# Hybrid decoder step on one core: filler projections spread by TensorE columns instead of by steps

## The chip, the cores and the metric

The kernel runs on one core of a Trainium2 chip. The metric is the time of one execution on the device in microseconds (us). Engines are called as in the profile: PE is the matrix engine (TensorE), PEld its weight loads, DVE is VectorE, ACT is ScalarE, POOL is GpSimd, SP is SyncE, which issues all the transfers (DMA) here.

## What is computed

Two layers of a decoder. Each normalises 1024 prompt rows and 64 sample rows of width 1024, multiplies them by one wide input matrix, and takes from the product queries, keys and values (8 heads of 64), gates, and the inputs of a second mixer. The first mixer is causal attention with a decay:

```
s = q k^T * scale + (c_q - c_k)      c = cumulative sum of log forget gates
s = -inf above the diagonal
p = softmax(s);  out = p v
m = sigmoid(g_a) * (a @ w_pa) + sigmoid(g_b) * (b @ w_pb);  x = x + m @ w_o
```

Everything is in f32 precision: an operand is split into a high and a low part, and a product is three matmuls (high by high, high by low, low by high) of at most 512 columns, in the helper `three` (L71, L72, L73).

## The kernel before

The program is a sequence of phases: constants, normalisation of rows, and then for each layer attention, spatial, branches, merge and output. The change touches one function, `attention_plan` (L461), which writes down by hand the order of the attention phase. Every engine walks through the same list of steps in `attention_phase` (L541) and does its own part of each, in that order; semaphores tie them together. The kinds of steps that matter:

- **T(h, G, j)**, **V(h, G, j)**: head h, query half G (512 queries), key block j. T transposes up to four 128x128 blocks of the softmax result (L1089). ACT copies them out of the bank as the high part (L810), DVE subtracts for the low part (L991). V multiplies by the values (L1102, L1103), LAG = 2 steps after its T. There are 96 of these steps for each layer, 12 for each head; "step n" below counts them from 0, so head h starts at step 12h. Step n issues T of step n and V of step n - 2.
- **S(h, i)**: scores of the query block i (L1072, L1074, L1077). DVE adds the decay and takes the maximum (L975), ACT does the exponential (L800), DVE normalises (L877). A chunk of scores waits on PE until DVE has taken the chunk two before it. S of head h + 1 goes beside T and V of head h.
- **O(h, G)**: after the last V of a group, ACT (L819) and DVE (L998) add the two halves of the result. The next group's first V (j = 0) waits for it on PE.
- **W(p, k)**: a weight tile for the heads of pair p: SP loads it (L653, L656), ACT makes the high part (L739), POOL the low part for even k (L838), DVE for odd k (L899). **Z(p, t)**: their projection, 24 matmuls of 384 columns, and **X(p, t)** its transposes (L1049). POOL works on each Z for its norm.
- **P(b, c, half)**: the filler. 16 blocks b of the merge gates, each of three column chunks c (384, 384 and 320 columns), are projected in two halves of 12 matmuls. After both halves ACT takes the tanh (**E**, L754), which frees the bank, and SP stores it (**D**, L679). 14 of the 96 halves run before step 0, and 82 beside the steps. Its weights come in **G** units, two for each b: SP loads them (L660, L662), ACT makes the high part (L746) and POOL the low part (L843).

W and G share a ring of NST = 4 staging slots. In the order of the plan, the load of unit u + 4 is issued when SP gets to unit u, and `load_w` (L646) first waits until unit u has been split into high and low. G units of block b + 2 come into the plan behind the last half of block b, so wherever that half is moved, they go along.

The filler is dealt out by the loop at the end of `attention_plan`. A half costs 1 and a Z costs 2; the other kinds cost nothing. After each step it adds halves until what was spent has caught up with an equal share for each step:

```
total = sum(2 * (s[0] == "Z") ...) + len(fill.pieces) - first
while spent + fill.at - first < total * (n + 1) / (len(steps) + 1) and ...:
    fill.half()
```

That is 54 for the 27 Z and 82 halves, 136 in all, or 1.4 for each step. Before a Z an open pair is closed by its second half (`before_z`, L449).

Of the kernel before, what the change touches and what calls it, by code (L numbers as in the profile page):

```python
# [26 lines left out]
KT = D // P  # L27
# [430 lines left out]
        self.spill(0)  # L458


def attention_plan():  # L461

    plan = [("W", 0, k) for k in range(KT)]
    fill = Filler(plan)
    for t in range(NT):  # L470
        plan.append(("Z", 0, t))
        if t:
            plan.append(("X", 0, t - 1))
        if t >= 3:
            fill.weights(min(t - 2, NF))
    plan += [("F",)]
    fill.chunk()
    plan += [("W", 1, k) for k in range(2)]
    fill.chunk()
    plan += [("X", 0, NT - 1), ("C",), ("N", 0)]  # L480
    for i in range(1, 4):
        plan += [("W", 1, k) for k in (2 * i, 2 * i + 1)]
        fill.chunk()
    fill.read(0)
    plan += [("S", 0, 0), ("S", 0, 1)]
    fill.half()
    plan += [("S", 0, 2)]
    fill.half()
    fill.read(0)
    plan += [("S", 0, 3)]  # L490
    fill.half()
    fill.half()
    after = {}
    PER = 12

    def put(n, *steps):
        after.setdefault(n, []).extend(steps)

    for h in range(H):
        if h:  # L500
            put(PER * (h - 1), ("N", h))
        for i, off in enumerate((-10, -9, -8, -6, -4, -3, -2, 0)):
            if h or i >= 4:
                put(max(0, PER * h + off), ("S", h, i))
    for p in range(1, PAIRS):
        at = [3, 5, 7, 9, 11, 13, 15, 17, 19]
        for t, n in zip(range(NT - len(at), NT), at):
            n += 2 * PER * (p - 1)
            put(n, ("Z", p, t))
            if t and ("X", p, t - 1) not in plan:  # L510
                put(n, ("X", p, t - 1))
        put(n + 2, ("X", p, NT - 1))
        if p + 1 < PAIRS:
            for k in range(KT):
                put(n + 1 + k // 2, ("W", p + 1, k))
    steps = [(h, G, j) for h in range(H) for G in range(2) for j in range(4 * G + 4)]
    first = fill.at
    total = sum(2 * (s[0] == "Z") for v in after.values() for s in v) + len(fill.pieces) - first
    spent = 0
    for n in range(len(steps) + LAG):  # L520
        if n < len(steps):
            plan.append(("T",) + steps[n])
        fill.read(0)
        if n >= LAG:
            plan.append(("V",) + steps[n - LAG])
            h, G, j = steps[n - LAG]
            if j == 4 * G + 3:
                plan.append(("O", h, G))
        for s in after.pop(n, []):
            if s[0] == "Z":  # L530
                fill.before_z()
                spent += 2
            plan.append(s)
        while spent + fill.at - first < total * (n + 1) / (len(steps) + 1) and fill.at < len(fill.pieces):
            fill.half()
    fill.end()
    assert not after
    return plan


def attention_phase(nc, l, g, sem):  # L541
    plan = attention_plan()
    R = Region(nc, "at", g.free_attention)
    S = lambda n: sem(f"a_{n}")
# [1513 lines left out]
```

How the kernel before makes its waits and increments, by code:

```python
        @block.sync  # L103
        def _(sp):
            for t in range(NT):
                if t >= NX:
                    sp.wait_ge(hn_r, t - NX + 1)
                    sp.wait_ge(ss_r, t - NX + 1)
                sp.dma_start(xt[0:ROWS[t], t % NX, :], x_rows(g, t)).then_inc(x_in[t % NX], 16)
                if t == 1:
                    sp.dma_start(gain[:, :], g.gains[0:1, :].to_broadcast([P, D])).then_inc(consts, 16)
# [1 line left out]
        @block.scalar  # L113
        def _(act):
            def evac(t):
                for b in range(2):
                    act.wait_ge(tr_r, t + 1)
                    nc.scalar.activation(g.h_hi[:, 4 * b:4 * b + 4, t * P:t * P + ROWS[t]],
                                         hps[t % 2][b][:, :].rearrange("p (k r) -> p k r", k=4)[:, :, 0:ROWS[t]],
                                         ACT.Copy).then_inc(h_hi, 1)
            for t in range(NT):
                act.wait_ge(x_in[t % NX], 16 * (t // NX + 1))
                if t:
                    act.wait_ge(ss_r, t)
                    if t >= 2:
                        act.wait_ge(ms_r, t - 1)
                nc.scalar.activation(sqj[0:ROWS[t], :], xt[0:ROWS[t], t % NX, :], ACT.Square,
                                     accum_out=ss[0:ROWS[t], t % 2:t % 2 + 1]).then_inc(ss_r, 1)
                if t:
                    evac(t - 1)
            evac(NT - 1)
# [12 lines left out]
        @block.vector  # L145
# [13 lines left out]
                if t:  # L159
                    evac(t - 1)
                dve.wait_ge(ss_r, t + 1)
                if t >= 2:
```

## Time and profile before

| what | value |
|---|---|
| median of three runs (2157.60 to 2164.94) | 2157.71 us |
| the profiled execution: its own time, its span | 2161.27 us, 2159.6 us |
| PE busy, share of the span | 1941.4 us, 90% |
| DVE, ACT, POOL busy | 981.4, 678.0, 486.1 us |
| mean granted clock of PE | 0.965 |
| filler matmuls (three lines), busy | 261.1 + 254.6 + 254.5 us |

The span is the time from the first to the last instruction of the profiled execution. Matmuls overlap and their ends are modelled, so busy time says where PE had something in hand, while the distance from start to start says how fast it went. A group's "idle before" is the time its engine stood before these instructions, with what released it. Idle time costs something only on the engine that sets the pace. The steps run from 159.4 to 578.4 us in layer 0 and from 1213.5 to 1629.7 us in layer 1.

### The profile page before, as it was taken

The page shows a single profiled execution, that of the slowest core. Times are in us where ns is not written, and L with a number is a line of the kernel's source. Part 1 is how long each engine was busy: PE and PEld are TensorE (multiplying, and loading weights), DVE is VectorE, ACT ScalarE, POOL GpSimd, SP SyncE. Part 2 cuts the span into 40 slices and gives each one's busy share as a digit, 9 for nine tenths or more (in the row PEclk, how much of TensorE's full clock was granted, in tenths as well). Part 3 has the DMA queues.
Part 4 walks back from the last instruction along what each step waited for, and adds up shares of the span by engine and source line. Part 5 has one row for each costly group of instructions (what it writes and reads, how often), then busy time and mean ns, then how long its engine had stood idle before and what let it go on. Part 6 is the DMA issues. An engine that isn't in the chain of part 4 may idle for free. (4 is left out here: it accounts for less than half of the span.)

```text
span 2159.6 us, 31030 instructions
## 1 busy us (share of the span) xinstructions
PE 1941.4 (90%) x11188; PEld 1780.0 (82%) x11188; DVE 981.4 (45%) x2322; ACT 678.0 (31%) x1487; POOL 486.1 (23%) x499
## 2 busy tenths in 40 slices
PE   2789989999896999898979898999997789989899
PEld 2689888999775889897859898989996588889876
DVE  3335646554255324444434365565533633344441
ACT  3233434444232322103223343443433232221020
POOL 0432323331111112202015132333211021121010
PEclk9999999999997999999989999999999899999999
DMA  2341231212213322433222313131212152214341
GB/s 92 71 102 43 57 80 51 78 52 78 77 47 93 112 83 67 156 108 127 103 63 59 103 47 81 48 92 49 70 47 81 39 152 84 72 51 154 107 166 59
DMA packets 215499, 178.38 MB, mean 83 GB/s; under 512 B 50004, under 2 KB 186724, under 8 KB 215348
## 3 DMA queue, kind: packets, MB, share of 16 engines
q1 hardware_dynamic: 215348, 176.41, 28.3%
q8 instruction: 90, 1.47, 0.3%
q14 instruction: 61, 0.50, 0.1%
HBM read 131.65 MB, written 44.71 MB: 82 GB/s over the span
## 5 line engine op out<-in xcount | busy, mean ns | idle before, releaser
L71 PE MATMUL bank<-keep_hhi,at_fhi 128*128 128x384 f32 (+1 forms) x768 | 261.1, 340 | 16.2 <-ACT at_th L754 16.2
L73 PE MATMUL bank<-keep_hhi,at_flo 128*128 128x384 f32 (+1 forms) x768 | 254.6, 331 | 0.0
L72 PE MATMUL bank<-keep_hlo,at_fhi 128*128 128x384 f32 (+1 forms) x768 | 254.5, 331 | 0.0
L71 PE MATMUL bank<-at_whi,keep_hhi 128*128 128x384 f32 (+3 forms) x576 | 201.3, 349 | 17.6 <-POOL at_wlo L838 17.5
L71 PE MATMUL bank<-keep_hhi,br_whi 128*128 128x384 f32 (+1 forms) x576 | 196.2, 341 | 20.6 <-POOL br_wlo L1109 20.6
L72 PE MATMUL bank<-at_wlo,keep_hhi 128*128 128x384 f32 (+3 forms) x576 | 198.0, 344 | 0.0
L73 PE MATMUL bank<-at_whi,keep_hlo 128*128 128x384 f32 (+3 forms) x576 | 197.7, 343 | 0.0
L72 PE MATMUL bank<-keep_hlo,br_whi 128*128 128x384 f32 (+1 forms) x576 | 189.7, 329 | 0.0
L73 PE MATMUL bank<-keep_hhi,br_wlo 128*128 128x384 f32 (+1 forms) x576 | 189.5, 329 | 0.0
L800 ACT ACTIVATE at_prob<-at_prob,at_nmx 128x128 f32<-128x128 f32 (+7 forms) x128 | 99.5, 777 | 280.4 <-DVE at_nmx L982 280.3
L991 DVE TENSOR_TENSOR at_ptlo<-bank,at_pthi 128x512 fp32r<-128x512 f32 x192 | 106.0, 552 | 157.6 <-ACT at_pthi L810 157.6
L71 PEld LDWEIGHTS bank<-keep_hhi,at_fhi 128*128 128x128 f32 x768 | 147.1, 191 | 19.8 <-ACT at_th L754 17.6
L72 PEld LDWEIGHTS bank<-keep_hlo,at_fhi 128*128 128x128 f32 x768 | 147.3, 192 | 0.8
L73 PEld LDWEIGHTS bank<-keep_hhi,at_flo 128*128 128x128 f32 x768 | 146.8, 191 | 0.0
L843 POOL TENSOR_TENSOR at_flo<-at_stage,at_fhi 128x512 fp32r<-128x512 f32 x64 | 82.0, 1292 | 241.5 <-ACT at_fhi L746 241.5
L71 PE MATMUL bank<-wo_whi,keep_hhi 128*128 128x512 f32 (+1 forms) x288 | 116.3, 404 | 14.2 <-POOL wo_wlo L1109 14.2
L71 PEld LDWEIGHTS bank<-keep_hhi,br_whi 128*128 128x128 f32 x576 | 109.5, 190 | 22.7 <-POOL br_wlo L1109 21.1
L71 PEld LDWEIGHTS bank<-at_whi,keep_hhi 128*128 128x128 f32 (+1 forms) x576 | 106.9, 186 | 23.7 <-POOL at_wlo L838 20.9
L810 ACT ACTIVATE at_pthi<-bank 128x512 fp32r<-128x512 f32 x192 | 93.7, 488 | 94.6 <-PE bank L1089 94.1
L72 PE MATMUL bank<-wo_wlo,keep_hhi 128*128 128x512 f32 (+1 forms) x288 | 115.1, 400 | 0.0
L73 PE MATMUL bank<-wo_whi,keep_hlo 128*128 128x512 f32 (+1 forms) x288 | 115.1, 400 | 0.0
L851 POOL TENSOR_TENSOR at_zg<-at_zc,at_gqk 128x256 f32<-128x256 f32 (+1 forms) x72 | 53.0, 736 | 266.4 <-ACT at_zc L763 266.4
(240 smaller groups left out, 4406.2 us busy)
## 6 DMA issues: line engine op xcount, KB each, us to landing
mg_gate<-gates SPq DMA_DIRECT2D x32, 544.0 KB, 7.0
at_stage<-in_w_in SPq DMA_DIRECT2D x128, 128.0 KB, 2.6
at_stage<-in_w_in SPq DMA_DIRECT2D x64, 192.0 KB, 2.7
gates<-at_th SPq DMA_DIRECT2D x64, 192.0 KB, 2.3
br_stage<-in_w_in SPq DMA_DIRECT2D x48, 256.0 KB, 3.2
at_decay<-ncum SPq DMA_DIRECT2D x16, 512.0 KB, 4.1
br_k<-in_cache_k SPq DMA_DIRECT2D x32, 256.0 KB, 3.0
br_v<-in_cache_v SPq DMA_DIRECT2D x32, 256.0 KB, 3.0
```

Source lines behind the costliest of these rows:

```text
L71: nc.tensor.matmul(out, sh, mh, start=start and i == 0, stop=False)
L72: nc.tensor.matmul(out, sh, ml, start=False, stop=False)
L73: last = nc.tensor.matmul(out, sl, mh, start=False, stop=stop and i == n - 1)
L800: nc.scalar.activation(prob[:, blk(i):blk(i) + w], prob[:, blk(i):blk(i) + w], ACT.Exp, bias=nmx[:, si % 2:si % 2 + 1], accum_out=sm[:, si ...
L810: nc.scalar.activation(pt_hi[:, ti % (LAG + 1), lo:512], tps[ti % 2][:, lo:512], ACT.Copy).then_inc(t_hi, 1)
L843: nc.gpsimd.tensor_tensor(flo[:, fu % NF, :], stage[:, units[s] % NST, :], fhi[:, fu % NF, :].bitcast(F32), ALU.subtract).then_inc(w_lo_p, 1)
L851: link(nc.gpsimd.tensor_tensor(zg[0:n, :].rearrange("p (s h d) -> p s h d", s=2, h=2), zc[0:n, zi % 2, 0:2 * P].rearrange("p (s h d) -> p ...
L991: nc.vector.tensor_tensor(pt_lo[:, ti % (LAG + 1), lo:512], tps[ti % 2][:, lo:512], pt_hi[:, ti % (LAG + 1), lo:512].bitcast(F32), ALU.sub ...
```

## The change

The halves are dealt out by columns that pass through PE, with every kind of step counted. The list of other steps, and their order among themselves, stays; only P and what hangs on it (E, D, G) moves.

```diff
+HALF = 12 * 384.0
+def cost(s):
+    if s[0] == "Z":
+        return 3 * KT * 384.0
+    if s[0] == "X":
+        return 4 * 240.0
+    if s[0] == "S":
+        return (s[2] // 4 + 1) * 2 * 400.0 + 128
+    if s[0] == "T":
+        h, G, j = s[1:]
+        return (4 - max(0, j - 4 * G)) * 200.0
+    if s[0] == "V":
+        h, G, j = s[1:]
+        return (4 - max(0, j - 4 * G)) * 2 * 128.0
+    return 0.0
...
-    total = sum(2 * (s[0] == "Z") for v in after.values() for s in v) + len(fill.pieces) - first
-    spent = 0
+    total = sum(cost(s) for v in after.values() for s in v) + sum(cost(("T",) + s) + cost(("V",) + s) for s in steps)
+    total += HALF * (len(fill.pieces) - first)
+    spent = 0.0
     for n in range(len(steps) + LAG):
         if n < len(steps):
             plan.append(("T",) + steps[n])
+            spent += cost(plan[-1])
         fill.read(0)
         if n >= LAG:
             plan.append(("V",) + steps[n - LAG])
+            spent += cost(plan[-1])
...
             if s[0] == "Z":
                 fill.before_z()
-                spent += 2
             plan.append(s)
-        while spent + fill.at - first < total * (n + 1) / (len(steps) + 1) and fill.at < len(fill.pieces):
+            spent += cost(s)
+        while spent + HALF * (fill.at - first) < total * (n + 1) / (len(steps) + 1) and fill.at < len(fill.pieces):
             fill.half()
```

Worked through, the total is 865,216 columns, and a step's share 8,920. Halves issued in each step (the same in both layers):

| steps | before | after |
|---|---|---|
| 0 to 7 | 2 1 2 1 0 0 0 0 | 1 2 1 0 1 1 0 0 |
| 8 to 19 | 1 1 0 0 1 1 0 0 0 0 1 1 | 0 0 1 1 0 0 0 0 1 1 0 0 |
| 20 to 27 | 0 1 2 1 2 1 1 0 | 0 1 2 1 2 1 2 1 |
| 28 to 37 | 1 1 0 0 1 1 0 0 0 0 | 0 0 1 1 0 0 0 0 0 0 |
| 38 to 44 | 1 1 0 0 1 1 0 | 1 1 0 0 1 1 0 |
| 45 to 51 | 1 1 2 1 2 1 0 | 0 2 1 2 1 2 0 |
| 52 to 67 | 1 1 0 0 0 0 1 1 0 0 1 1 0 0 0 0 | 1 1 0 0 0 0 0 0 1 1 0 0 1 1 0 0 |
| 68 to 71 | 1 2 1 1 | 0 1 1 2 |
| 72 to 95 | 35 in all, 1 or 2 each | 38 in all, 1 to 3 each |

Z stands in every second step from 3 to 19, 27 to 43 and 51 to 67. The two G units of b = 6 move from step 23 to step 24, behind W(2, 7), which stays in step 23. Those of b = 8 move from step 43, ahead of all W(3, k) (steps 44 to 47), to step 46, between W(3, 5) and W(3, 6); with 4 staging slots the load of W(3, 6) is then issued at W(3, 4) and no longer at W(3, 2), and that of W(3, 7) at W(3, 5) and no longer at W(3, 3).

## Rows read from the trace of the kernel before

**Rows 1.** Stretches: us, busy (count) of PE PEld DVE ACT POOL, PEclk, DMA, GB/s

```profile
159.40:578.40 419.00, 402.64 (x2465) 384.14 (x2463) 219.18 (x636) 168.94 (x396) 115.45 (x113) 0.99 0.23 62
1213.50:1629.70 416.20, 401.19 (x2466) 382.68 (x2464) 219.07 (x636) 168.94 (x396) 115.42 (x113) 0.99 0.23 62
```

**Rows 2.** Waits of PE in the first stretch: total us, times, longest us

```profile
PE bank L1102 <- DVE at_ao L998: 7.1, 7, 3.0
PE bank L1072 <- DVE at_mx L975: 6.8, 8, 1.4
PE bank L71 <- ACT at_th L754: 2.5, 1, 2.5
```

**Rows 3.** The same view, second stretch

```profile
PE bank L1102 <- DVE at_ao L998: 7.0, 7, 3.0
...
PE bank L71 <- ACT at_th L754: 0.9, 1, 0.9
```

**Rows 4.** Timeline of PE: start us, us, engine, line, operation [idle before <-releaser]

```profile
270.84 0.39 PE L71 MATMUL bank<-keep_hhi,at_fhi 128*128 128x384 f32 x1
...
272.98 0.34 PE L71 MATMUL bank<-keep_hhi,at_fhi 128*128 128x384 f32 x1
```

**Rows 5.** Timeline of PE at score steps, without and with work between them

```profile
370.57 0.47 PE L1072 MATMUL bank<-at_qk 128*128 128x512 f32 x1 [1.17 <-DVE at_mx L975]
...
419.58 0.40 PE L1103 MATMUL bank<-at_ptlo,at_vsplit 128*128 128x512 f32 x1
421.40 0.47 PE L1072 MATMUL bank<-at_qk 128*128 128x512 f32 x1 [1.42 <-DVE at_mx L975]
...
474.25 0.40 PE L1103 MATMUL bank<-at_ptlo,at_vsplit 128*128 128x512 f32 x1
474.48 0.40 PE L1072 MATMUL bank<-at_qk 128*128 128x512 f32 x1
```

**Rows 6.** Timeline of PE at the first value product of a group

```profile
242.75 0.47 PE L1102 MATMUL bank<-at_pthi,at_vsplit 128*128 128x512 f32 x1 [0.80 <-DVE at_ao L998]
...
445.50 0.47 PE L1102 MATMUL bank<-at_pthi,at_vsplit 128*128 128x512 f32 x1 [1.10 <-DVE at_ao L998]
...
463.31 0.47 PE L1102 MATMUL bank<-at_pthi,at_vsplit 128*128 128x512 f32 x1 [0.31 <-DVE at_ao L998]
```

**Rows 7.** Timeline of all engines, 271 to 284 us, head 2 of layer 0

```profile
271.07 0.38 SPq L660 DMA_DIRECT2D at_stage<-in_w_in  x1
...
271.59 1.20 DVE L899 TENSOR_TENSOR at_wlo<-at_stage,at_whi 128x392 fp32r<-128x392 f32 x1
...
274.17 0.63 ACT L746 ACTIVATE at_fhi<-at_stage 128x512 fp32r<-128x512 f32 x1 [2.71 <-DMA at_stage<-in_w_in]
...
276.75 0.63 ACT L746 ACTIVATE at_fhi<-at_stage 128x512 fp32r<-128x512 f32 x1 [1.95 <-DMA at_stage<-in_w_in]
...
278.25 0.44 PE L71 MATMUL bank<-keep_hhi,at_fhi 128*128 128x384 f32 x1 [2.52 <-ACT at_th L754]
...
283.78 0.76 PE L1102 MATMUL bank<-at_pthi,at_vsplit 128*128 128x512 f32 x1 [2.96 <-DVE at_ao L998]
```

**Rows 8.** Stretch table at the low granted clock

```profile
283.20:290.00 6.80, 6.22 (x20) 5.96 (x21) 1.76 (x7) 0.83 (x5) 0.00 (x0) 0.50 0.24 71
1338.00:1341.40 3.40, 3.40 (x13) 3.31 (x12) 0.59 (x4) 0.82 (x4) 0.00 (x0) 0.51 0.18 61
```

**Rows 9.** Timeline of all engines, 375 to 392 us, heads 3 and 4

```profile
375.28 0.47 PE L1072 MATMUL bank<-at_qk 128*128 128x512 f32 x1 [0.36 <-DVE at_mx L975]
...
382.90 2.65 POOL L838 TENSOR_TENSOR at_wlo<-at_stage,at_whi 128x392 fp32r<-128x392 f32 x2 [3.88 <-ACT at_whi L739]
...
383.68 0.95 ACT L739 ACTIVATE at_whi<-at_stage 128x392 fp32r<-128x392 f32 x2
...
384.77 1.20 DVE L899 TENSOR_TENSOR at_wlo<-at_stage,at_whi 128x392 fp32r<-128x392 f32 x1
...
391.77 0.47 PE L1102 MATMUL bank<-at_pthi,at_vsplit 128*128 128x512 f32 x1 [0.49 <-DVE at_ao L998]
```

## The prediction

> **What bounds the kernel now.** I read the stretch table first, for the attention steps alone. PE is busy for 402.6 of 419.0 us in layer 0 and 401.2 of 416.2 in layer 1, while DVE has work for about 219 [rows 1]. So PE sets the pace and only some 16 and 15 us of each stretch are open to a new order: moving halves cannot shorten PE's own work. Next I read who PE waits for: seven waits for DVE's sum of the two output halves (V with j = 0, behind O), eight for DVE's reading of a score bank, and one for a tanh that frees the filler's bank [rows 2, 3]. Everything outside the attention phase is issued as before, so it costs nothing either way: no cover of it is touched.
>
> The profiled execution took 2161.27 us with a span of 2159.6; the median of three is 2157.71. The sum is made against the profiled execution and then put on the median, 3.56 us lower.
>
> **What a half is worth.** One half starts at 270.84 and the next at 272.98, so a 384-column half takes 2.14 us of PE [rows 4]. All 82 are still issued. What counts is what PE waits for where one is gone, and which wait is covered where one has come. A wait costs a little more than its listed idle time, as ends are modelled: from the second V matmul to the scores it is 1.82 us with an idle time of 1.42, and 0.23 us without a wait, so 1.59 are lost, 0.17 more than listed [rows 5]. I add 0.2 to every listed wait.
>
> **Scores behind scores.** In steps 8 and 32 the half goes that stands between S(h, 4) and S(h, 5), with a Z ahead of both. Steps 56 and 57 have this very order already: PE is through with its V at once and waits 1.42 us for DVE, which is still at the Z's share. That makes 1.6 us at each of the two places. In step 68 it is the same with the shorter last Z (64 rows); the like place after step 44 waited 1.17 [rows 5], so 1.4. Sum **+4.6** for each layer.
>
> **Values behind O.** With a Z but no half since the last step but one, the first V of the next group waited 1.10 us in step 62 and 0.80 in step 18 [rows 6]; where halves stand in both steps ahead (steps 12 and 13, ahead of step 14) there is no wait. The change takes the halves of 12 and 13 away (+1.3 in step 14), and gives two to 16 and 17 (-1.0 in step 18) and to 60 and 61 (-1.3 in step 62). One wait of 0.31 goes in step 66 [rows 6] and one of the same kind comes in step 30. Sum **-1.0**.
>
> **Head 2, steps 24 to 27.** Here is the longest idle time. ACT reaches the G units of b = 6 before their loads have landed and stands for 2.71 and 1.95 us; the tanh, the copies of T and O queue behind it, and PE idles 2.52 us ahead of P(5, 1, 0) and 2.96 ahead of V(2, 0, 0) [rows 7]. In layer 1 the first is 0.9, the second again 3.0 [rows 3]. The change puts these units a step later, behind the exponential of S(2, 7). Then T(2, 0, 0) is copied at once. DVE is done with W(2, 7) at 271.59 + 1.20 = 272.8 [rows 7]. From the like point of heads 3 and 4 (384.77 + 1.20 = 385.97) to the first V (391.77) it took 5.8 us [rows 9]; two G copies and a tanh now lie in this chain, 2 x 0.63 [rows 7] and about 0.5, so V(2, 0, 0) starts at 272.8 + 5.8 + 1.75 = 280.3. PE gets there at about 277.9, so it waits 2.4 where it lost 2.7 + 3.2. That is **-3.5** in layer 0 and, from 1.1 + 3.2, **-1.9** in layer 1. The granted clock fell to its lower level (0.50 of 2.4 GHz) for 6.8 us in layer 0 and 3.4 us in layer 1, right behind this idle time [rows 8]. At half speed such a stretch loses half of itself, less the idle part: 3.1 and 1.7. With one wait of 2.4 us left I count 0.3 of it as still there: **-2.8** and **-1.4**.
>
> **Heads 3 and 4, steps 45 to 50.** The half behind S(4, 5) goes. S(4, 6) waits for DVE to read S(4, 5), which hangs on DVE's queue (copy of T, split of W), not on PE; it starts at 375.28 after a wait of 0.36 [rows 9] and would start then with one half less done: **+2.1**. Then the weights. W(3, 6) is now loaded only when W(3, 4) is split. POOL's two splits from 382.90 take 2.65 us together [rows 9], so the first ends at 384.2. A load needed 3.1 us from its issue (271.07) to its use (274.17), the next one was ready 2.6 later [rows 7]. So W(3, 6) is there at about 387.4 and W(3, 7), issued 0.9 later, at 388.3 at the earliest and 390.0 at the latest; I take 388.3, as this stretch has no stores of Z beside it. ACT copies them at 383.68 today, without a wait [rows 9]. Behind ACT's wait stand the copy of T(4, 0, 0), the exponential of S(4, 7), the copy of T(4, 0, 1), one tanh and O; DVE waits at W(3, 7) with the low parts and the scores behind it. POOL and SP wait too, but what they hold (loads of b = 10, the decay row of head 5) is needed later. DVE's split ends at 388.3 + 0.5 + 1.2 = 390.1 and no longer at 385.97; with the 5.8 us chain and the tanh, V(4, 0, 0) starts at 396.4. PE has done the same number of halves by then as before (six since S(4, 6)), so it arrives at 391.0 as today and waits 5.4 us where it lost 0.7: **+4.6**. The clock: an idle time of this length should let it fall. The stretches above cost 1.7 and 3.1 [rows 8]; I take 2.0 here and 0.8 for the 2.7 us ahead of S(4, 6): **+2.8**.
>
> The Trainium skill, page "DMA: Bandwidth & Descriptors", section "Anatomy of one DMA — SWDGE (gpsimd) path", gives a transfer about 2.0 us and its bytes at 436 GB/s, which would be an estimated 2.45 us for such a load; that is for another issuing path. By it both loads would land 0.65 us sooner and the sum be about 1.3 us smaller.
>
> **Sum.** Layer 0: 4.6 - 1.0 - 3.5 - 2.8 + 2.1 + 4.6 + 2.8 = +6.8. Layer 1: 4.6 - 1.0 - 1.9 - 1.4 + 2.1 + 4.6 + 2.8 = +9.8. Together +16.6: the profiled execution would take 2177.9 us, and the median **2174.3 us**, 0.77% slower. A change within 0.5% (10.8 us) is about what a measurement of this kernel can't tell from none.
>
> **Bounds.** The landing of W(3, 7) is worth 1.7 us more in each layer if late and 0.5 less if early. The clock is worth from 0 to 3.1 at each place; from no fall at either place to one of 3.1 at both: -2.8 to +3.4. Two layers: 2167.7 to 2184.5.
>
> **Rivals.** (a) *The weights come in time.* If ACT has other work until the loads land, or V(4, 0, 0) is held by nothing new, 4.6 and the 2.0 of clock fall away in each layer: +3.4 in all, 2161.1 us. For it speaks that no wait of ACT for W shows at these steps today, against it that the ring's slot is freed only at 384.2 and the use is at 383.7 today. (b) *The two old clusters only change places*, with all smaller waits as before: 2157.7 us, or what amounts to the change not doing what it says, since Z and the weight steps keep their places and the halves shift by one to four steps. (c) *Faster.* DVE's lag behind a Z, 1.42 us at S, decides. Should it be gone when fewer tanhs and stores run beside it, neither the score waits (4.6), nor S(4, 6) (2.1), nor head 4 (4.6 and 2.8) come, and what is saved in head 2 stays: 16.6 - 2 x 14.1 = -11.6, 2146.1 us. It needs a lag under some 0.2 us. Against it: the lag comes from DVE's and ACT's own instructions, which don't change, and was there at each of eight S waits [rows 2]. (d) *Slower still*: the second load comes 1.7 us late, the clock falls at three places in each layer for 3.1 each instead of 3.1 in all (counting the 0.3 in head 2): 16.6 + 2 x (1.7 + 6.2) = +32.4, 2190.1 us.
>
> **Chances.** The forecast 0.65; (a) 0.14, (b) 0.09, (c) 0.05, (d) 0.07. Below 10.8 us of change lie (a), (b) and a small part of the forecast's own range (0.04 of it): same 0.27, faster 0.05, slower 0.68. The range takes in the forecast's bounds and (b) with a little scatter, and stops short of (c) and of the far end of (d): 2156 to 2186.
>
> **What would show it.** In the profile after: no wait of ACT for the load of at_fhi and 2.4 us of PE idle, not 5.5, in head 2; PE's clock at 1.0 there; new waits of L1072 for L975 of 1.4 us in steps 9, 33 and 69; 2.5 us or more ahead of S(4, 6); ACT's L739 waiting 2 to 4 us for a load of at_stage, and a wait of some 5 us at L1102 for L998 in head 4, the longest in the steps, with a fall of the clock beside it. The forecast is wrong if that last wait is under 2 us, or if PE's idle time in the steps grows by less than 3 us in each layer.

## The result and the profile after

The change makes the kernel slower: 2174.69 us median against 2158.7 for the kernel before on the same chip, a ratio of 1.007, with a 95% interval of 1.0051 to 1.0089. The profiled execution of after took 2173.97 us with a span of 2172.3, against 2161.27 and 2159.6 before. So the forecast (2174.3 us, 0.77% slower) held; by the medians the change costs 16.0 us, by the two profiled executions 12.7.

First the stretch table of after, for the steps of layer 0 and of layer 1, and three short stretches in layer 0 at the low granted clock. The columns are those of [rows 1].

```profile
160.30:584.90 424.60, 403.52 (x2465) 384.67 (x2464) 219.00 (x636) 168.33 (x396) 115.48 (x113) 0.99 0.22 61
1219.60:1643.10 423.50, 403.00 (x2464) 384.19 (x2463) 218.95 (x636) 168.44 (x396) 115.53 (x113) 0.99 0.22 61
371.10:374.50 3.40, 3.40 (x12) 3.22 (x13) 1.63 (x6) 2.79 (x7) 0.74 (x1) 0.50 0.40 93
391.60:395.00 3.40, 3.40 (x15) 3.40 (x14) 0.91 (x5) 0.49 (x2) 0.00 (x0) 0.50 0.51 154
333.60:337.00 3.40, 3.40 (x13) 3.30 (x12) 1.78 (x8) 0.49 (x2) 1.94 (x2) 0.50 0.28 60
```

The steps are 424.6 and 423.5 us long where they were 419.0 and 416.2 [rows 1]: +5.6 and +7.3, 12.9 together, where the whole span grew by 12.7 (the rest of the program is the same within 0.3). PE's busy time grew by under 2 us, as half clock stretches count as busy; the rest is waiting. The low clock of head 2 [rows 8] is gone and stands now at heads 3 and 4.

Who PE waits for in the first stretch of after (total us, times, longest):

```profile
PE bank L1096 <- DVE at_mx L999: 13.5, 11, 2.5
PE bank L1126 <- DVE at_ao L1022: 7.5, 6, 2.5
```

L1096, L1126 and L71 of after are L1072, L1102 and L71 of before. The score waits were 6.8 us in eight and are 13.5 in eleven; the V waits are 7.5 where they were 7.1; the wait for a tanh is gone [rows 2]. The timeline of PE in layer 0 of after shows each kind once (S(1, 5), V(1, 0, 0), V(2, 0, 0), V(3, 0, 0), S(4, 6), V(4, 0, 0)):

```profile
203.71 0.47 PE L1096 MATMUL bank<-at_qk 128*128 128x512 f32 x1 [1.42 <-DVE at_mx L999]
...
228.50 0.47 PE L1126 MATMUL bank<-at_pthi,at_vsplit 128*128 128x512 f32 x1 [1.11 <-DVE at_ao L1022]
...
277.63 0.47 PE L1126 MATMUL bank<-at_pthi,at_vsplit 128*128 128x512 f32 x1 [1.41 <-DVE at_ao L1022]
...
332.31 0.47 PE L1126 MATMUL bank<-at_pthi,at_vsplit 128*128 128x512 f32 x1 [2.06 <-DVE at_ao L1022]
...
371.05 0.70 PE L1096 MATMUL bank<-at_qk 128*128 128x512 f32 x1 [2.47 <-DVE at_mx L999]
...
391.03 0.47 PE L1126 MATMUL bank<-at_pthi,at_vsplit 128*128 128x512 f32 x1 [2.47 <-DVE at_ao L1022]
```

Behind the last of them lie ACT, POOL and DVE at the weights of heads 3 and 4 (same kernel, same layer):

```profile
374.13 1.07 DVE L923 TENSOR_TENSOR at_wlo<-at_stage,at_whi 128x392 fp32r<-128x392 f32 x1 [0.60 <-ACT at_whi L763]
...
379.04 1.36 DVE L923 TENSOR_TENSOR at_wlo<-at_stage,at_whi 128x392 fp32r<-128x392 f32 x1
...
382.77 0.53 ACT L763 ACTIVATE at_whi<-at_stage 128x392 fp32r<-128x392 f32 x1 [2.24 <-DMA at_stage<-in_w_in]
383.38 1.04 POOL L862 TENSOR_TENSOR at_wlo<-at_stage,at_whi 128x392 fp32r<-128x392 f32 x1 [0.58 <-ACT at_whi L763]
...
384.10 0.53 ACT L763 ACTIVATE at_whi<-at_stage 128x392 fp32r<-128x392 f32 x1 [0.79 <-DMA at_stage<-in_w_in]
...
384.66 0.57 DVE L923 TENSOR_TENSOR at_wlo<-at_stage,at_whi 128x392 fp32r<-128x392 f32 x1 [4.06 <-ACT at_whi L763]
```

ACT copies W(3, 6) and W(3, 7) only when their loads land, and DVE stands 4.06 us for the second, where before it went straight on [rows 9].

To say how much each step cost I took, in both traces, the time from the start of each of its items to the start of the next, less what an item of that kind takes when nothing holds it. This gives the loss of PE by step, waits and half clock together (us, before to after):

| step | what is lost there | layer 0 | layer 1 |
|---|---|---|---|
| 9, 33, 69 | S behind S | 0.13, 0.13, 0.18 to 1.86, 1.85, 1.67 | the same to 1.84, 1.84, 1.66 |
| 14 | V(1, 0, 0) | 0.01 to 1.35 | 0.01 to 1.33 |
| 18, 62, 66 | V of a group | 1.10, 1.45, 0.55 to 0.01 each | 1.07, 1.45, 0.55 to 0.01 each |
| 25 to 27 | head 2 | 9.10 to 1.95 | 6.18 to 1.95 |
| 38, 39 | V(3, 0, 0) | 1.58 to 4.10 | 1.58 to 2.54 |
| 46 | S(4, 6) | 0.67 to 4.40 | 0.67 to 4.31 |
| 50 | V(4, 0, 0) | 0.84 to 4.38 | 0.84 to 4.22 |
| 86 | V(7, 0, 0) | 0.11 to 0.51 | 0.11 to 0.43 |

Step 0 is given apart, as its four scores wait for each other in every kernel: from the start of T(0, 0, 0) to the first half it takes 8.2 us in before and 7.6 in after in layer 0 (159.39 to 167.59, 160.34 to 167.93), and 8.3 in both in layer 1.

### The profile page after: what moved, and what is told of

It is laid out like the page before. It is cut to its first block and busy times, and to the rows that moved or that the text cites. A ratio compares the mean times of both kernels' runs of the same rounds, so it can differ in the third digit from the quotient of the medians.

```text
span 2172.3 us, 31030 instructions
## 1 busy us (share of the span) xinstructions
PE 1941.7 (89%) x11188; PEld 1779.5 (82%) x11188; DVE 979.7 (45%) x2322; ACT 677.0 (31%) x1487; POOL 486.9 (22%) x499
## 5 line engine op out<-in xcount | busy, mean ns | idle before, releaser
L71 PE MATMUL bank<-keep_hhi,at_fhi 128*128 128x384 f32 (+1 forms) x768 | 262.8, 342 | 13.1 <-ACT at_th L778 13.1
L71 PE MATMUL bank<-at_whi,keep_hhi 128*128 128x384 f32 (+3 forms) x576 | 200.1, 347 | 18.6 <-POOL at_wlo L862 17.9
L71 PE MATMUL bank<-keep_hhi,br_whi 128*128 128x384 f32 (+1 forms) x576 | 196.1, 341 | 20.5 <-POOL br_wlo L1133 20.5
L71 PEld LDWEIGHTS bank<-keep_hhi,at_fhi 128*128 128x128 f32 x768 | 148.9, 194 | 16.2 <-ACT at_th L778 14.2
L71 PE MATMUL bank<-wo_whi,keep_hhi 128*128 128x512 f32 (+1 forms) x288 | 115.8, 402 | 14.1 <-POOL wo_wlo L1133 14.1
L71 PEld LDWEIGHTS bank<-keep_hhi,br_whi 128*128 128x128 f32 x576 | 109.4, 190 | 22.6 <-POOL br_wlo L1133 21.1
L71 PEld LDWEIGHTS bank<-at_whi,keep_hhi 128*128 128x128 f32 (+1 forms) x576 | 106.2, 184 | 24.0 <-POOL at_wlo L862 20.3
```

What stands on the lines that cost most here:

```text
L71: nc.tensor.matmul(out, sh, mh, start=start and i == 0, stop=False)
```

## The experiments

Eleven kernels were run in three groups, each group on one chip with its own runs of the kernel before; ratios are to that. Each expectation spells out what its theories say. A is in most of them the working of the prediction, by which each loss belongs to the item named for it (in experiment 4 that is B, in the last three D). B is otherwise the rival of the text in question. C came up after the fifth kernel and stands in the last three. "Losses" are those of the table above.

**1. The two G units of b = 8 behind the exponential of S(4, 7)**, everything else as in after, so that W(3, 6) and W(3, 7) are loaded as early as before.

```
 # after, behind fill.end()
+units = [("G", 16), ("G", 17)]
+plan = [s for s in plan if s not in units]
+at = plan.index(("P", 7, 1, 0)) + 1      # end of step 48
+plan[at:at] = units
```

> The changed kernel, with only the two weight units of filler block 8 moved from step 46 to the end of step 48, behind the exponential of S(4,7), so that W(3,6) is loaded at W(3,2) again. Theory A (late loads): ACT's two waits for at_stage at W(3,6) and W(3,7), 2.2 and 0.8 us, go; the wait ahead of V(4,0,0), 2.7 us, falls to about 1, the clock doesn't fall behind it, and each layer saves about 3 us, 6 in all (span near 2166). Theory B (only one half stands between V(3,1,7) and V(4,0,0), where there were two): the wait stays at 2.5 us or more and the time stays within 1 us.

Measured: 2169.52 us, 1.0033 (1.0023 to 1.0043). Steps 419.6 and 419.5 us. In its timeline of PE, the first scores of group 1, S(4, 6) and V(4, 0, 0):

```profile
361.49 0.40 PE L1100 MATMUL bank<-at_qk 128*128 128x512 f32 x1
...
369.08 0.76 PE L1100 MATMUL bank<-at_qk 128*128 128x512 f32 x1 [2.46 <-DVE at_mx L1003]
...
386.51 0.47 PE L1130 MATMUL bank<-at_pthi,at_vsplit 128*128 128x512 f32 x1 [0.16 <-DVE at_ao L1026]
```

The wait ahead of V(4, 0, 0) is 0.16 where it was 2.47, and the half clock behind it is gone: step 50 loses 0.51 where it lost 4.38. S(4, 6) still waits 2.46. Theory A had 3 us less in each layer; it was 4 to 5. So the place of two small units, through the loads that queue behind them, was worth some 4 us in each layer.

**2. The same kind of edit on the kernel before**: the G units of b = 6 at the end of step 24, halves untouched.

```
 # before, behind fill.end()
+units = [("G", 12), ("G", 13)]
+plan = [s for s in plan if s not in units]
+at = plan.index(("D", 14)) + 1
+plan[at:at] = units
```

> The kernel before, with only the two weight units of filler block 6 moved from step 23 to the end of step 24. Theory A (what was gained in head 2 comes from these units' place alone): the wait ahead of P(5,1,0), 2.5 and 0.9 us, goes, that ahead of V(2,0,0) falls from 3.0 to about 1.5, the clock doesn't fall there; 7 us less in layer 0 and 4 in layer 1, so a span near 2148 and a ratio near 0.995. Theory B (the halves' own new places gained it): within 2 us of before.

Measured: 2153.29 us, 0.9953 (0.9941 to 0.9965). V(2, 0, 0) and the stretch of layer 0, from its timeline and stretch table:

```profile
279.74 0.47 PE L1106 MATMUL bank<-at_pthi,at_vsplit 128*128 128x512 f32 x1 [1.50 <-DVE at_ao L1002]
```

```profile
159.50:571.70 412.20, 399.59 (x2465) 381.25 (x2463) 219.06 (x636) 169.02 (x397) 115.80 (x113) 1.00 0.24 63
```

Head 2 lost 9.1 and 6.2 us and loses 2.0 in each layer, with the granted clock at 1.00 over the stretch. What the change gains in head 2 is this move alone; no half had to move for it.

**3. The halves back where a score step needs one.** The loop is replaced by a list of halves for each step, which is that of after but for steps 8 to 11, 30 to 33, 68 and 71.

```
-        while spent + HALF * (fill.at - first) < total * (n + 1) / (len(steps) + 1) and fill.at < len(fill.pieces):
+        while fill.at - first < sum(HALVES[:n + 1]):
             fill.half()
 # 8 to 11: 0 0 1 1 -> 1 1 0 0; 30 to 33: 1 1 0 0 -> 0 0 1 1; 68: 0 -> 1; 71: 2 -> 1
```

> The changed kernel, with a half put back between S(h,4) and S(h,5) in steps 8 and 32 (with its partner in 9 and 33, taken from 10, 11, 30 and 31) and one in step 68 (taken from 71). Theory A: the three waits of L1096 for L999, 1.4, 1.4 and 1.2 us, go and nothing takes their place: 4.9 us less in each layer, near 10 in all (span near 2162.5). Theory B (DVE's lag only moves to the next group): less than 4 us in all, with longer waits at the V that follow.

Measured: 2166.0 us, 1.0015 (1.0005 to 1.0026). The waits of PE in layer 0:

```profile
PE bank L1099 <- DVE at_mx L1002: 8.9, 8, 2.5
PE bank L1129 <- DVE at_ao L1025: 6.6, 6, 2.5
```

Score waits are eight again, 4.6 us less in all. The losses of steps 9, 33 and 69 went back to 0.13, 0.11 and 0.18. V(3, 0, 0) went back too: its listed wait is 1.11 again where after has 2.06, as two halves stand between S(3, 4) and V(3, 0, 0) again and PE comes there later. That answers to the 1 us which the prediction had not seen. The steps are 417.9 and 418.0 us long.

**4. One half from step 46 to step 45**, behind S(4, 5), where before had it.

```
 # after with HALVES; 45: 0 -> 1; 46: 2 -> 1
```

> The changed kernel, with one of the two halves of step 46 put back into step 45, between S(4,5) and S(4,6). Theory A (DVE's chain and the late loads fix when V(4,0,0) starts): the wait ahead of S(4,6) falls from 2.5 to 0.4 us and the clock doesn't fall there, but what the clock gives back is lost again as a longer wait ahead of V(4,0,0), near 4 us; only the half itself is gained, 2.1 us in each layer, 4.2 in all (span near 2168). Theory B (the waits add up freely): 3.7 us in each layer, 7.4 in all (span near 2165).

Measured: 2178.43 us, 1.0068 (1.0052 to 1.0084). S(4, 6) and V(4, 0, 0) in its timeline of PE:

```profile
370.48 0.47 PE L1099 MATMUL bank<-at_qk 128*128 128x512 f32 x1 [0.68 <-DVE at_mx L1002]
...
390.64 0.77 PE L1129 MATMUL bank<-at_pthi,at_vsplit 128*128 128x512 f32 x1 [4.63 <-DVE at_ao L1025]
```

The wait at S(4, 6) went from 2.47 to 0.68 and that at V(4, 0, 0) from 2.47 to 4.63; step 46 loses 0.98 in place of 4.40, step 50 loses 7.19 in place of 4.38, and both stretches are as long as in after or longer (424.7 each). Nothing was won, where the two theories had 2.1 and 3.7 us in each layer. A wait that is filled without anything crossing the next one is only handed on.

**5. Experiments 1 and 4 together.** No new lines beside theirs.

> Both edits of e1 and e4 in the changed kernel: the weight units of filler block 8 behind step 48, and a half back in step 45. e4 alone gained nothing, since no half had moved across V(4,0,0), whose start the late loads fixed. Theory A (with the loads early, DVE's chain from S(4,6) sets V(4,0,0), and a half between S(4,5) and S(4,6) is done for nothing): the waits ahead of S(4,6) and V(4,0,0) come to about 0.6 and 0.7 us as in the kernel before, no fall of the clock in steps 45 to 50; against e1 3.3 us less in each layer, span near 2162. Theory B (V(4,0,0) is fixed by something else): the time of e1, within 2 us of a span of 2168.7.

Measured: 2176.61 us, 1.0075 (1.0059 to 1.0092): a clear miss, a loss beside experiment 1 (1.0033) where a gain was expected. Its timeline of PE and stretch table:

```profile
363.80 0.40 PE L1103 MATMUL bank<-at_qk 128*128 128x512 f32 x1
...
388.84 0.77 PE L1133 MATMUL bank<-at_pthi,at_vsplit 128*128 128x512 f32 x1 [3.22 <-DVE at_ao L1029]
```

```profile
388.50:391.90 3.40, 3.06 (x11) 2.90 (x12) 1.18 (x6) 0.75 (x3) 0.39 (x1) 0.50 0.96 284
391.90:395.30 3.40, 3.40 (x15) 3.40 (x14) 0.34 (x2) 0.63 (x1) 0.63 (x1) 0.51 0.39 136
```

The loads are early, so V(4, 0, 0) starts 25.0 us behind S(4, 4), just as in experiment 1 (361.49 to 386.51). What PE no longer waits at S(4, 6) (3.2 us of loss less) it waits at V(4, 0, 0) (3.3 more); and behind this wait the clock is low for 6.8 us, in which the first items of step 50 lose 2.8 us.

**What these five say together (theory C).** From S(4, 4) to V(4, 0, 0) runs a chain of DVE and ACT: scores read, exponentials, low parts, splits of W, tanh, O, the sum at at_ao. It has a length of its own. PE's items in it take 5.9 us and 2.14 for each half [rows 4]; the rest of the length is lost, wherever inside it shows. (Two of the halves inside have 320 columns and take about 1.8 us; the 5.9 allows for them. In experiments 9 and 10 it is three, and 5.55.) Measured in layer 0, with the same chain in head 2:

| kernel, head | S(h, 4) to V(h, 0, 0), us | halves inside | PE loses |
|---|---|---|---|
| before, 2 | 29.26 | 7 | 8.41 |
| before, 4 | 24.10 | 7 | 3.24 |
| after, 2 | 25.00 | 7 | 4.15 |
| after, 4 | 27.57 | 6 | 8.80 |
| 1, head 4 | 25.02 | 6 | 6.24 |
| 3, head 4 | 27.53 | 6 | 8.77 |
| 4, head 4 | 27.78 | 6 | 9.01 |
| 5, head 4 | 25.04 | 6 | 6.26 |

(27.57 - 5.9 - 6 x 2.14 = 8.8 for after; 24.10 - 5.9 - 7 x 2.14 = 3.2 for before.) The half of experiment 4 moved inside the chain, so the loss stayed. What the edit of the spreading rule did was to move one half out of the chain of head 4, behind V(4, 0, 0), and to lengthen the chain by 3.5 us.

This holds for heads 2 and 4, which have the W splits and no Z in the span. In head 3, with three Z in it, the same span follows the halves (26.25 us with two in before, 24.67 with none in after), so its length is not set by the other engines.

**6. Experiments 1, 3 and 4 together**, as one kernel.

> The changed kernel with the edits of e1, e3 and e4 together; what remains of the change is the place of the block 6 units, and halves moved to 16, 17, 60, 61, 64, 65. Theory A (the three costs are separate and sum up): about 12 us less lost than in the changed kernel in each layer (3.9, 4.9 with 1 at V(3,0,0), 3.4): a span near 2149, ratio to the kernel before near 0.995, like e2. Theory B (they overlap): span above 2155.

Measured: 2159.26 us, 0.9999 (0.9989 to 1.001), where 2149 was hoped for. Steps 415.6 and 415.5 us. The chain of head 4 is 25.04 with six halves and loses 6.29, as in 5. Experiment 4's edit gains nothing, and the gains of 1 and 3 come but for 1.5 us in each layer: steps 46 and 50 together lose 6.1 where they lose 4.6 in experiment 1, since most of the waiting stands ahead of V(4, 0, 0) again and the clock falls behind it (0.50 from 383.1 to 386.5).

**7. Only the late loads, put into the kernel before**: the G units of b = 8 between W(3, 5) and W(3, 6), halves of before.

```
 # before, behind fill.end()
+units = [("G", 16), ("G", 17)]
+plan = [s for s in plan if s not in units]
+at = plan.index(("W", 3, 5)) + 1
+plan[at:at] = units
```

> The kernel before, its halves untouched, with only the two weight units of filler block 8 moved from step 43 to step 46, between W(3,5) and W(3,6). Theory A (late loads alone cost it): ACT waits about 2 and 1 us for at_stage at W(3,6) and W(3,7), the wait ahead of V(4,0,0) grows from 0.7 to near 4 us, the clock falls behind it: 4 to 6 us in each layer, span near 2169, ratio near 1.0045. Theory B (it needs the missing halves too): ratio under 1.002.

Measured: 2171.27 us, 1.0049 (1.0032 to 1.0066). The chain of head 4 grew from 24.10 to 27.67 (27.64 in layer 1) with its seven halves; step 50 loses 5.63 and 3.26 where it lost 0.84, step 49 a further 0.9. So the late loads cost without any half moved. The stretches grew by 7.8 and 1.6 us. Theory A had 4 to 6 in each layer and a span near 2169; the profiled one is 2169.3. Layer 0: some 6.4 in steps 48 to 51 (of these 1.9 behind V(4, 0, 0), by the clock) and 1.6 at step 0. Layer 1: 3.6 in steps 48 to 50, less 1.9 in head 2, whose order is not changed: what head 2 loses varies from one execution to the next.

**8. A version made by these rules from the kernel before.** No step's place but that of halves and G units is changed.

```
 # before with HALVES
 # a pair from each of 18, 38, 58, 62 to 16, 36, 56, 60; a new pair in 64, 65;
 # one half from 26 to 20 and one from 50 to 44; one less in 77 and in 87
+for units, last in (([("G", 12), ("G", 13)], ("T", 2, 0, 1)), ([("G", 18), ("G", 19)], ("T", 4, 0, 1))):
+    plan = [s for s in plan if s not in units]
+    at = plan.index(last)
+    plan[at:at] = units
```

> The kernel before with the halves dealt out by a list, put where PE waits: pairs from 18, 38, 58 and 62 to 16, 36, 56 and 60, a new pair at 64, one half from 26 to 20 and one from 50 to 44, two fewer after step 76; the weight units of blocks 6 and 9 behind S(2,7) and S(4,7). Theory A (each wait is covered by a half ahead of it): the waits of 0.8 to 1.4 us in steps 18, 21, 38, 45, 57, 62 and 66 go, head 2's too; 17 us less in layer 0 and 14 in layer 1, span near 2129, ratio near 0.986. Theory B (DVE and ACT are then what bounds these steps, and the waits come back one step later): less than half of that, ratio above 0.993.

Measured: 2133.16 us, 0.9869 (0.9852 to 0.9886). Steps 405.6 and 404.0 us, 13.4 and 12.2 less than in before, where theory A had 17 and 14. The chains of heads 2 and 4 are 25.07 and 25.01 long and hold eight halves, and lose 2.0 to 2.1.

**9. One half from step 50 to step 45 in after**: now one does cross V(4, 0, 0).

```
 # after with HALVES; 45: 0 -> 1; 50: 2 -> 1
```

> The changed kernel, with one half taken from step 50, behind V(4,0,0), and put into step 45. e4 moved one within the stretch from S(4,4) to V(4,0,0) and gained nothing. Theory C (that stretch is one chain through DVE and ACT, 24.1 us in the kernel before, 27.6 with the late loads, and PE's wait is what of it the halves inside don't fill, wherever they stand in it): the stretch stays at 27.6 us, and with seven halves inside in place of six the waits of steps 46 and 50 together fall by 2.1 us, 2 to 3 us less in each layer, span near 2167.5. Theory D (each wait stands for itself): the wait of S(4,6) falls by 2.1 us and the clock no longer falls ahead of V(4,0,0), whose wait stays at 2.7: 3.7 us in each layer, span near 2165.

Measured: 2173.54 us, 1.0064 (1.0046 to 1.0082).

```profile
361.83 0.40 PE L1099 MATMUL bank<-at_qk 128*128 128x512 f32 x1
...
389.30 0.47 PE L1129 MATMUL bank<-at_pthi,at_vsplit 128*128 128x512 f32 x1 [3.24 <-DVE at_ao L1025]
```

389.30 - 361.83 = 27.47: the length stands, with seven halves it loses 6.94 in place of 8.80, and layer 0 is 1.9 us shorter than in after. Layer 1 is only 0.7 shorter; there the clock fell behind V(3, 0, 0), where it had not in after. By theory C 2 to 3 us in each layer were expected.

**10. The same, and the G units of b = 8 behind O**, at the end of step 49.

```
 # experiment 9, and behind fill.end()
+units = [("G", 16), ("G", 17)]
+plan = [s for s in plan if s not in units]
+at = plan.index(("P", 7, 2, 0)) + 1
+plan[at:at] = units
```

> As e9, and the two weight units of filler block 8 out of the chain altogether, to the end of step 49 behind O(3,1). Theory C: the stretch from S(4,4) to V(4,0,0) is back at 24.1 us with seven halves inside, the waits of S(4,6) and V(4,0,0) at 0.6 and 0.7 us, no fall of the clock: 7 us less than the changed kernel in each layer, span near 2158, ratio near 1.000. Theory D: as e9 plus the 3.9 us that e1 gained in each layer, the same total by another road; so the lengths of the stretch in e9 and e10 tell the two apart, not the time here.

Measured: 2164.52 us, 1.002 (1.0008 to 1.0032). The chain is 24.10 us long in layer 1, with step 50 at 0.85. In layer 0 it is 25.31, and the timeline of PE and ACT says why:

```profile
363.37 0.40 PE L1103 MATMUL bank<-at_qk 128*128 128x512 f32 x1
...
386.70 0.49 ACT L785 ACTIVATE at_th<-bank 128x384 f32<-128x384 f32 x1 [1.18 <-DMA gates<-at_th]
387.21 0.59 ACT L850 ACTIVATE at_ao<-bank 64x512 f32<-64x512 f32 x1
...
388.68 0.47 PE L1133 MATMUL bank<-at_pthi,at_vsplit 128*128 128x512 f32 x1 [1.71 <-DVE at_ao L1029]
```

A tanh ahead of O's copy waits 1.18 us until a store has read its buffer: 24.10 + 1.18 = 25.28. The steps are 5.6 and 6.7 us shorter than in after, where 7 were expected, and the time stays above the expected 1.000.

**11. Experiment 8 with both pairs of G units behind O**, and the pair of halves of steps 42, 43 in 40, 41.

```
 # experiment 8, with
-([("G", 12), ("G", 13)], ("T", 2, 0, 1)), ([("G", 18), ("G", 19)], ("T", 4, 0, 1))
+([("G", 12), ("G", 13)], ("T", 2, 0, 3)), ([("G", 18), ("G", 19)], ("T", 4, 0, 3))
```

> As e8, with the weight units of blocks 6 and 9 behind O, out of the chain to V(2,0,0) and V(4,0,0) (in e8 they stood between the exponential and O), and the pair of steps 42 and 43 in 40 and 41. Theory C: both chains are about 1 us shorter, the waits ahead of V(2,0,0) and V(4,0,0) fall from 1.6 and 1.5 to 0.6 and 0.5 us, that of step 42 from 1.0 to 0: about 3 us less in each layer than e8, ratio near 0.984. Rival: the copies were hidden behind DVE's work, and the time stays at e8's ratio of 0.987.

Measured: 2131.06 us, 0.9863 (0.9845 to 0.988), the best, though no further below experiment 8 than the intervals allow. Its timeline of PE, its waits and its stretch table, all of layer 0:

```profile
355.62 0.40 PE L1079 MATMUL bank<-at_qk 128*128 128x512 f32 x1
...
379.73 0.47 PE L1109 MATMUL bank<-at_pthi,at_vsplit 128*128 128x512 f32 x1 [0.33 <-DVE at_ao L1005]
```

```profile
PE bank L1079 <- DVE at_mx L982: 2.9, 3, 1.4
PE bank L1109 <- DVE at_ao L1005: 0.9, 3, 0.4
```

```profile
161.10:561.80 400.70, 396.67 (x2465) 380.72 (x2463) 219.03 (x636) 168.70 (x398) 115.53 (x113) 1.00 0.24 65
```

The chain is 24.11 us (379.73 - 355.62) and loses about 1.1 with eight halves. Outside step 0 PE loses 2.9 us less in each layer than in experiment 8, which is what theory C had. PE is busy for 396.7 of 400.7 us, with 3.8 us of listed waits where before had 16.4 [rows 2]. In layer 1 the stretch is some 2 us longer, all of it in step 0, where the clock fell (0.50 from 1201.0 to 1207.8) and in layer 0 did not; that hides part of the gain in the time.

## Why the prediction was right, and which term was off

The total was right in direction and size, and by the terms that carried it, but that it agrees to 0.4 us is luck. The steps grew by 12.9 us in the traces where the sum has 16.6. V(4, 0, 0) and head 2 came out smaller than forecast, and a loss at V(3, 0, 0) that was not seen makes up for part of it. The rest is scatter: the four times of after span 4.2 us and the four of before 7.3, and their medians happen to lie 16.0 apart. Forecast and measured, by layer:

| step of the prediction | forecast | layer 0 | layer 1 |
|---|---|---|---|
| scores behind scores | +4.6 | +4.9 | +4.9 |
| values behind O | -1.0 | -1.7 | -1.7 |
| head 2, waits and clock | -6.3 / -3.3 | -7.2 | -4.2 |
| S(4, 6), V(4, 0, 0) and clock | +9.5 | +7.3 | +7.0 |
| V(3, 0, 0) | 0 | +2.5 | +1.0 |
| V(7, 0, 0), step 0 | 0 | -0.2 | +0.3 |
| steps in all | +6.8 / +9.8 | +5.6 | +7.3 |

- *Scores behind scores* was right in place and size (1.42 listed, 1.7 lost at steps 9 and 33), and experiment 3 took all three back by giving the halves back.
- *Values behind O*: the four places of steps 14, 18, 62 and 66 behave as said; the wait at step 30 that would have cost 0.3 did not come, and step 66 gave back 0.5 instead of 0.3.
- *Head 2*: the mechanism was right, as experiment 2 shows alone. ACT finds the loads of G there: its two copies start at once behind the exponential (trace of after, 274.31), with no wait. The wait ahead of V(2, 0, 0) is 1.41 listed and not 2.4, because the two G copies and the tanh do not add 1.75 us to the chain: with the G units in it the chain is 25.0 where without it is 24.1, so 0.9. And the clock stayed up, so nothing of its cost was left.
- *Heads 3 and 4*: the loads landed as forecast: ACT's copy of W(3, 7) started 13.05 us behind S(4, 6) (371.05 to 384.10), the forecast being 388.3 - 375.28 = 13.0. **The term that was mis-sized is V(4, 0, 0), +4.6 (its own figures, 5.4 less 0.7, give 4.7); it measured +2.0** (+1.8 in layer 1), three steps of its working being off. DVE's split took 0.57 us, not 1.2, as POOL's own had ended at 384.42. The tanh was not on the chain: ACT did it from 388.98 to 389.46, while DVE normalised, and from the split's end (385.23) to V (391.03) it is the 5.8 us of before. And PE did not "arrive at 391.0 as today": the half clock behind S(4, 6), from 371.1 to 374.5, made it 1.7 us later. That half clock loss lies inside a chain whose length DVE and ACT set, so it was counted twice: once as clock, once in the wait it shortens. S(4, 6) was right (2.0 for 2.1), the clock roughly so (0.8 + 0.9 behind S(4, 6) and 1.6 behind V(4, 0, 0), 3.3 for 2.8).
- *Not seen*: V(3, 0, 0), 1 us more in each layer. Two halves are gone between S(3, 4) and V(3, 0, 0), and the forecast has a price only for the scores behind S(3, 4) (experiment 3 gives both back). In layer 0 there is a fall of the clock behind it, 1.4 us; in layer 1 the clock did not fall behind the same wait. V(7, 0, 0) adds 0.4 and 0.3. Against them, at step 0 of layer 0 the clock fell in the trace of before (163.8 to 167.2) and not in that of after: 0.6 us that no edit explains.
- *The signs*: the wait ahead of V(4, 0, 0) was to be some 5 us and the longest. It is 2.47, level with S(4, 6), and not far above the 2 us under which the forecast called itself wrong. ACT waits 2.24 and 0.79 us for the two loads where 2 to 4 was said. PE's idle time in the steps (length less busy) grew by 4.7 and 5.5 us, over the 3 that were asked for.
- *The rivals*: (a), the weights in time, is what experiment 1 makes of the change: its steps are 0.6 and 3.4 us longer than those of before where (a) has 0.2 and 3.2, so the total of (a) fits a kernel with early loads, and the change is not one. Its parts fit less well: V(3, 0, 0) is in none of them, and head 2 came out smaller. (b) is excluded by the eleven score waits. (c) needed DVE's lag to vanish; it is 1.42 us, as before. Of (d) only the fall at V(3, 0, 0) came, in one layer.
- *The figure of the Trainium skill* (page "DMA: Bandwidth & Descriptors", section "Anatomy of one DMA — SWDGE (gpsimd) path"): 2.0 us and the bytes at 436 GB/s, an estimated 2.45 us, would have had both loads ready 0.65 us earlier than the 3.1 us taken from the rows. In the trace W(3, 6) was issued at 380.00 and used at 382.77, W(3, 7) at 380.94 and 384.10: 2.8 and 3.2 us, so the time from the rows is the nearer one. The two are for different issuing paths.

## What to carry to other kernels

An even spread of filler by cost is not better than one by number of steps if it does not know where the waits are (here it was 0.7% worse): find the spans whose length another engine's chain sets, measure them between two anchors, and count how much work PE has inside; an item moved within such a span gains nothing, one moved into it gains its duration as long as that much of the span is left (here up to eight halves, which left about 1.1 us). Outside such spans each wait wants a half ahead of it, as at the scores behind a Z. What is left over goes where PE waits for nothing. Before moving a small unit that holds a slot of a staging ring, look which load is issued when that slot comes free, and what stands in order behind the instruction that will wait for it: here two G units behind W(3, 5) cost 3.5 us of chain in each layer, and two others behind an exponential gave 4 to 7 back. Waits that are given as separate terms must be checked for lying in one span, half clock included.

## What the runs showed of the hardware that was not expected

- DVE's subtraction of two 128x392 tiles takes 0.57 us with POOL idle (each of the eight such in after), and 1.07, 1.36 and 1.20 us beside the same operation of POOL (374.13 and 379.04 in after; [rows 9]). With the second price on the path, a split may be cheaper where both engines are not at it together. The Trainium skill, page "GPSIMD Engine Reference", section "Specifications", says that POOL's SBUF interfaces are shared with VectorE's, with contention where a DVE instruction has two SBUF inputs, as this one has; the trace agrees.
- A fall of the clock costs by where it lies. In experiment 1 the clock fell at S(4, 6) (3.4 us from 368.6), inside the chain, which is none the longer for it (25.02 us, and 25.04 in experiment 5, where it did not fall there). In experiment 5 the same total of waiting stood in one piece at the chain's end, the clock fell behind it for 6.8 us from 388.4, and 2.8 us were lost in each layer on top.
- Behind the same wait of 2.06 to 2.08 us at V(3, 0, 0) the clock fell in some layers and not in others; each such fall cost 1.4 to 1.6 us of PE. It went together with step 0. Six kernels have this wait (after and experiments 1, 4, 5, 9 and 10). In seven of their twelve layers the clock had not fallen in the scores of step 0 (7.6 us from T(0, 0, 0) to the first half), and in all seven it fell behind V(3, 0, 0). In the other five it had fallen there (8.2 to 8.3 us), and in none of them did it fall behind V(3, 0, 0). Why the two go together is open; no run was made to tell.
